# Context pass of the gated MLP: SiLU, product and rounding through PSUM, and row dots placed behind two merges

## The chip, the core and the metric

The kernel runs on one core of one Trainium2 chip. The metric is the device time of one launch, in microseconds (us). Five engines run their own instruction queues in order and wait for each other through semaphores: TensorE (PE, the matrix engine), VectorE (DVE), ScalarE (ACT), GpSimd (POOL) and SyncE (SP, here only a queue of transfers). SBUF is the working memory, PSUM the eight banks into which PE accumulates.

## The reference, cut to what matters

Two layers work on 1024 latent tokens and 256 context tokens, width 1024. The stage that is changed is the gated MLP of layer 0, which both kinds of tokens pass:

```python
def _conv_ffn(u, w_up, conv_w, w_down):
    gate, val = jnp.split(_dwconv3(u @ w_up, conv_w), 2, axis=-1)
    return (jax.nn.silu(gate) * val) @ w_down
```

`_dwconv3` is a depthwise convolution of width 3 over the tokens. The hidden width is 2816, which is 22 blocks of 128 (`FT`). Beside it the layer-1 modulation `silu(c) @ ada_w[1]` is computed, 64 row dots of 1024 by 1024 numbers each ("row dots").

## The kernel before, in words

`split_ffn_phase` is one of the phases that follow each other, each with one instruction list for each engine. Every float32 product is made of three passes of rounded operands: weights high times activation high, weights high times activation low, weights low times activation high. "High" is the rounded value, "low" the remainder that the rounding left. So each weight block is loaded, rounded by ACT (`c_high`, L2407) and its remainder is formed by POOL (L2230) or, for one block in three (`c_by_dve`), by DVE (L2553).

**The context pass** runs first. `C_STEPS` lists 66 products in the order gate f, value f, down f-1, each of 24 matmuls. The gate and value products of block f go in turn into three PSUM banks (`UP_BANKS`), of which they use columns 0 to 255. For each f, before the change: ACT scales the gate result by the centre tap into `c_gate` (L2418), DVE adds the two side taps (L871, L873), ACT makes SiLU in place in `c_gate` (L2421), ACT and DVE do the same for the value in `c_value` (L2424, L871, L873), DVE multiplies both into `c_value` (L2542), DVE casts the product into `c_act_hi` (L2546) and subtracts to get `c_act_lo` (L2548). These feed the down product one round later. `c_gate` and `c_value` exist once, so ACT holds the next centre tap until `c_mul` (L2418) or `c_ready` (L2424). For f = 1 to 16 a quarter of the norm work for the latent tokens (`dve_sums`, L1814 to L1844) stands on DVE behind the value step, and a few casts on ACT.

**The latent pass** follows: `ITEMS` is up 0, up 1, up 2, down 0, then up, up, down for nine groups, at last up 21, down 9 and the end. An up item is seven block products P1, P7, P6, P2, P5, P4, P3 of 12 matmuls, which DVE merges: U2 (L2568, needs P6), U3 (L2572, needs P7 and U2), C22 (L2576, P5), C21 (L2579, P4), C12 (L2582, P3). P4 reuses the bank of P7 and waits for U3; P3 waits for C22. If an up follows directly on an up, the elementwise tail of the one before is still pending: gate taps, `gated` (L2596), `rounded` (L2604) and `low` (L2608) stand on DVE around the first merges of the next. Each item also carries two row dots, a and b: ACT issues the load of a row tile into one single buffer (`act_load`, which waits until the dot before is done), and DVE multiplies and sums it (`dve_dot`, L1903). POOL forms the weight remainders (L2199) and the block sums (L2213 to L2224) through all of this.

## Time and profile before

| | us |
|---|---|
| median of three runs | 3247.65 (3243.78 to 3250.87) |
| the profiled execution | 3248.8 |
| its span | 3247.0 |
| context pass, first to last matmul | about 414.6 to 640 |
| latent pass of the same phase | about 640 to 1345 |
| PE busy over the span | 2983.1 (92%) |
| DVE busy | 2046.4 (63%) |
| ACT busy | 1174.5 (36%) |
| POOL busy | 1308.9 (40%) |
| mean granted TensorE clock | 0.964 of full |

The shares are means over stages of different kind. The views used are the waits (who waited for whom), the busy time by windows, and the order of single instructions in time. In a time line the first number is the start from the span's start, the second the length of the instruction or of the run of them (xN), and what stands in brackets is the idle time of the engine just before it and the instruction that ended it. A row by tile gives the shortest, median and longest length in ns.

### The profile page before, as it was taken

Reading aid. Unit: us, or ns where it says so; the run is one execution under the profiler, and the core shown is the slowest. Engines: PE = TensorE matmul, PEld = TensorE weight load, DVE = VectorE, ACT = ScalarE, POOL = GpSimd, SP = SyncE. Lnnn points to the kernel's source line nnn. Section 1 sums busy time; section 2 is a strip of 40 time slices with the busy share of each in tenths; the row PEclk is TensorE's granted clock in tenths of the full one; section 3 lists DMA queues with packets and bytes.
Section 4 is the critical chain, followed back from the end, with each engine's and each line's share of the span. In section 5 each row is a group of like instructions: output and inputs, shape, how many; then the busy total and the mean of one; then the engine's idle time right before and its main releaser. Section 6 shows DMA issues by size and latency. Waiting matters only on the chain. (4 is left out here: it accounts for less than half of the span.)

```text
span 3247.0 us, 67120 instructions
## 1 busy us (share of the span) xinstructions
PE 2983.1 (92%) x28494; PEld 2440.6 (75%) x28494; DVE 2046.4 (63%) x2839; ACT 1174.5 (36%) x2178; POOL 1308.9 (40%) x834
## 2 busy tenths in 40 slices
PE   6998998989999999889989979999987899999999
PEld 4655888877777777668877757777876678888887
DVE  4513489877777777831226757777765666656656
ACT  4011244332332233320025656666642433233232
POOL 3212054567766777343311100000004366566664
PEclk9998999999999999989989989999998999999999
DMA  5431044422233233212311011111012011111112
GB/s 233 151 120 39 27 132 155 163 94 89 97 104 101 88 104 104 72 65 78 106 63 57 16 35 29 30 32 38 24 36 96 22 57 57 48 52 65 39 52 78
DMA packets 135914, 247.36 MB, mean 76 GB/s; under 512 B 9537, under 2 KB 97985, under 8 KB 135490
## 3 DMA queue, kind: packets, MB, share of 16 engines
q1 hardware_dynamic: 97314, 193.92, 17.8%
q10 hardware_dynamic: 38304, 49.16, 4.4%
q8 instruction: 227, 3.72, 0.5%
q14 instruction: 69, 0.57, 0.1%
HBM read 221.15 MB, written 21.89 MB: 75 GB/s over the span
## 5 line engine op out<-in xcount | busy, mean ns | idle before, releaser
L1353 POOL TENSOR_TENSOR f_w_lo<-h,f_w_hi 128x512 fp32r<-128x512 f32 x92 | 139.2, 1522 | 149.4 <-ACT f_w_hi L1561 149.4
L3916 POOL TENSOR_TENSOR rw_inv_k<-rw_ss_k,rw_expo 128x4 f32<-128x4 f32 x20 | 20.2, 1010 | 440.0 <-ACT rw_ss_k L4219 440.0
L2199 POOL TENSOR_TENSOR f_w_lo<-f_u_hi_raw,f_w_hi 128x512 fp32r<-128x512 f32 x86 | 142.6, 1670 | 119.4 <-ACT f_w_hi L2440 119.4
L2230 POOL TENSOR_TENSOR c_lo<-c_raw,c_hi 128x1024 fp32r<-128x1024 f32 x45 | 110.9, 2484 | 195.5 <-ACT c_hi L2407 195.4
L2199 POOL TENSOR_TENSOR f_w_lo<-f_w_raw,f_w_hi 128x512 fp32r<-128x512 f32 x84 | 143.3, 1714 | 105.5 <-ACT f_w_hi L2440 105.5
L1429 PE MATMUL ps<-u_hi,f_w_hi 128*128 128x512 f32 x440 | 173.3, 394 | 9.2 <-DVE f_value L1674 4.3
L1429 PE MATMUL ps<-u_lo,f_w_hi 128*128 128x512 f32 x440 | 172.8, 393 | 0.0
L1429 PE MATMUL ps<-u_hi,f_w_lo 128*128 128x512 f32 x440 | 172.7, 392 | 0.0
L1353 POOL TENSOR_TENSOR f_w_lo<-f_w_raw,f_w_hi 128x512 fp32r<-128x512 f32 x84 | 126.5, 1515 | 96.2 <-ACT f_w_hi L1561 96.2
L167 PE MATMUL ps<-u_hi,w_hi 128*128 128x512 f32 x552 | 145.4, 370 | 6.5 <-ACT cd_stage L1027 6.5
L2327 PE MATMUL ps<-wn_t_hi,f_w_hi 128*128 128x512 f32 x264 | 112.1, 424 | 38.8 <-DVE f_value L2572 38.8
L167 PE MATMUL ps<-u_lo,w_hi 128*128 128x512 f32 x552 | 141.7, 363 | 0.0
L167 PE MATMUL ps<-u_hi,w_lo 128*128 128x512 f32 x552 | 141.5, 362 | 0.0
L155 POOL TENSOR_TENSOR w_hi<-w_raw,zero 128x1024 fp32r<-128x1024 f32 x28 | 54.6, 1950 | 211.5 <-PE ps L167 186.9
L2327 PE MATMUL ps<-u_hi,f_w_hi 128*128 128x512 f32 x352 | 137.0, 389 | 0.0
L871 DVE SCALAR_TENSOR_TENSOR cd_stage<-ps,small,cd_stage 128x1023 f32<-128x1023 f32 (+1 forms) x24 | 21.2, 883 | 183.8 <-ACT cd_stage L1020 183.3
L2327 PE MATMUL ps<-u_hi,f_w_lo 128*128 128x512 f32 x352 | 137.0, 389 | 0.0
L2327 PE MATMUL ps<-u_lo,f_w_hi 128*128 128x512 f32 x352 | 137.0, 389 | 0.0
L167 PEld LDWEIGHTS ps<-u_hi,w_hi 128*128 128x128 f32 x552 | 93.2, 190 | 47.5 <-issue 31.9
L4537 DVE TENSOR_TENSOR rw_px<-ps,rw_level 128x256 f32<-128x256 f32 x200 | 82.2, 417 | 73.8 <-PE ps L4088 73.3
L1903 DVE SCALAR_TENSOR_TENSOR h<-h 128x1024 f32<-128x1024 f32 x64 | 108.7, 1698 | 31.1 <-DMA h<-in_ada_rows 31.1
L2288 PE MATMUL ps<-u_hi,c_hi 128*128 128x256 f32 x352 | 102.9, 292 | 16.5 <-DVE c_lo L2553 16.5
(525 smaller groups left out, 9518.0 us busy)
## 6 DMA issues: line engine op xcount, KB each, us to landing
c_raw<-in_ffn SPq DMA_DIRECT2D x66, 512.0 KB, 3.5
f_w_raw<-in_ffn SPq DMA_DIRECT2D x64, 512.0 KB, 4.3
h<-in_ada_rows ACTq DMA_DIRECT2D x64, 512.0 KB, 3.9
h<-in_ffn SPq DMA_DIRECT2D x34, 512.0 KB, 4.8
f_u_hi_raw<-in_ffn SPq DMA_DIRECT2D x32, 512.0 KB, 4.9
ada_ring_s<-in_ada SPq DMA_DIRECT2D x22, 512.0 KB, 3.3
w_raw<-in_cd_in SPq DMA_DIRECT2D x20, 512.0 KB, 4.3
z_scratch<-cd_stage ACTq DMA_DIRECT2D x15, 640.0 KB, 5.5
```

The lines of the kernel that those rows point to most:

```text
L155: pool.tensor_tensor(hi, K.raw[:, raw, :], K.zero[:, 0:1].to_broadcast([P, KT * P]), ALU.add).then_inc(self.hi_done, 1)
L167: mm = pe.matmul(K.ps[:, slot, c, 0:width], wt[:, s, w], x[:, k, at:at + width], start=start and n == 0, stop=stop and n == 2)
L871: chain.link(dve.scalar_tensor_tensor(cv[:, at + 1:at + n], psum[:, at:at + n - 1], w0, cv[:, at + 1:at + n], ALU.mult, ALU.add))
L1353: pool.tensor_tensor(two(w_lo[n % RING]), source(x), two(w_hi[n % RING]), ALU.subtract).then_inc(w_split, 1)
L1429: mm = pe.matmul(o, wt, xt, start=t in OPENS and j == 0 and i == 0, stop=j == HK - 1 and i == 2, skip_group_check=t not in OPENS)
L1903: dve.scalar_tensor_tensor(self.tile, self.tile, 1.0, self.cond, ALU.mult, ALU.mult, accum_out=self.K.mod[:, 1, t, c:c + 1]).then_inc(self ...
L2199: pool.tensor_tensor(two(w_lo[n % RING][:, :]), source(x), two(w_hi[n % RING][:, :]), ALU.subtract).then_inc(w_split, 1)
L2230: pool.tensor_tensor(c_lo[n % LOWS][:, :], c_raw[n % LOWS][:, :], c_hi[n % HIGHS][:, :], ALU.subtract).then_inc(c_lo_pool, 1)
L2288: mm = pe.matmul(o, wt[:, w], x[:, k, gap], start=k == 0 and q == 0, stop=k == KT - 1 and q == 2)
L2327: mm = pe.matmul(o, wt, xt, start=t in OPENS and j == 0 and i == 0, stop=j == HK - 1 and i == 2, skip_group_check=t not in OPENS)
L3916: pool.tensor_tensor(R.inv[:, :], R.ss[:, :], R.expo[:, :], ALU.pow).then_inc(inv_done, 1)
L4537: dve.tensor_tensor(PX[:, s].rearrange("p (b h) c -> p b h c", b=2), banks(s)[:, :, 0:128].rearrange("p b (h c) -> p b h c", h=2), R.level ...
```

## The change

In the context pass SiLU is written to columns 256 to 511 of the gate's bank and the product to the same columns of the value's bank, so that both live in PSUM. The cast to `c_act_hi` moves from DVE to ACT. DVE's own remainder of a weight block comes ahead of the remainder of the activations. The waits follow: ACT's centre tap of the gate waits only for the SiLU before, that of the value for the product before, and PE's gate and value products wait for `c_ready` of two rounds before and `c_mul` of the round before, instead of `c_conv`. The split of the weight remainders (two of three on POOL) is as it was. In the latent pass the first row dot of an up item moves from before U2 to behind `low`, ahead of C22, and ACT issues the load of the second row tile at step P4 instead of P5.

```diff
+    def c_silu_at(f):
+        s, b = UP_BANKS[2 * f % UPS]
+        return K.ps[:, s, b, CTX:2 * CTX]
+
+    def c_gated(f):
+        s, b = UP_BANKS[(2 * f + 1) % UPS]
+        return K.ps[:, s, b, CTX:2 * CTX]
...
-                    if u >= UPS:
-                        pe.wait_ge(c_conv, u - UPS + 1)
+                    if kind == "gate" and f >= 2:
+                        pe.wait_ge(c_ready, f - 1)
+                    elif kind == "value" and f >= 1:
+                        pe.wait_ge(c_mul, f)
...
-                        pe.wait_ge(c_conv, 2 * FT)
+                        pe.wait_ge(c_ready, FT)
...
-                    act.wait_ge(c_mul, f)
+                    act.wait_ge(c_silu, f)
                     act.activation(c_gate[:, :], c_up(f, 0), ACT.Identity, scale=tap(1, 0, f)).then_inc(c_centre, 1)
...
-                    act.activation(c_gate[:, :], c_gate[:, :], ACT.Silu).then_inc(c_silu, 1)
+                    act.activation(c_silu_at(f), c_gate[:, :], ACT.Silu).then_inc(c_silu, 1)
                     act.wait_ge(c_done, n + 1)
-                    act.wait_ge(c_ready, f)
+                    act.wait_ge(c_mul, f)
...
+                if kind == "value":
+                    act.wait_ge(c_mul, f + 1)
+                    if f >= 2:
+                        act.wait_ge(c_done, C_NTH["down", f - 2] + 1)
+                    act.copy(c_act_hi[f % 2][:, :], c_gated(f)).then_inc(c_act_hi_done, 1)
...
                     if t == P5:
                         c11(n)
+                    if t == P4:
                         rows.act_load(act, b)
...
-                    dve.tensor_tensor(c_value[:, :], c_value[:, :], c_gate[:, :], ALU.mult).then_inc(c_mul, 1)
-                    dve.wait_ge(c_mul, f + 1)
-                    if f >= 2:
-                        dve.wait_ge(c_done, C_NTH["down", f - 2] + 1)
-                    dve.tensor_copy(c_act_hi[f % 2][:, :], c_value[:, :]).then_inc(c_act_hi_done, 1)
-                    dve.wait_ge(c_act_hi_done, f + 1)
-                    dve.tensor_tensor(c_act_lo[f % 2][:, :], c_value[:, :], c_act_hi[f % 2][:, :],
-                                      ALU.subtract).then_inc(c_ready, 1)
+                    dve.tensor_tensor(c_gated(f), c_value[:, :], c_silu_at(f), ALU.mult).then_inc(c_mul, 1)
                 if n + HIGHS < C_ALL and c_by_dve(n + HIGHS):
...
+                if kind == "value":
+                    dve.wait_ge(c_act_hi_done, f + 1)
+                    dve.tensor_tensor(c_act_lo[f % 2][:, :], c_gated(f), c_act_hi[f % 2][:, :],
+                                      ALU.subtract).then_inc(c_ready, 1)
...
-                    rows.dve_dot(dve, a)
                     merge(n, U2)
                     merge(n, U3)
                     if pending is not None:
                         low(pending)
+                    rows.dve_dot(dve, a)
                     merge(n, C22)
```

## Rows read from the trace of the kernel before

**Rows 1.** Windows: length, busy (count) of PE, PEld, DVE, ACT, POOL; clock; DMA.
```profile
472.00:494.00 22.00, 19.30 (x152) 18.17 (x151) 21.58 (x24) 10.72 (x16) 10.53 (x5) 1.00 0.47 154
604.00:626.00 22.00, 21.96 (x184) 22.00 (x185) 21.51 (x23) 11.12 (x16) 12.66 (x6) 1.00 0.60 197
837.20:840.10 2.90, 2.90 (x8) 2.32 (x7) 1.04 (x2) 1.21 (x2) 1.00 (x1) 0.50 0.87 291
842.00:856.00 14.00, 14.00 (x62) 11.44 (x61) 12.74 (x11) 3.99 (x4) 7.90 (x4) 1.00 0.34 112
```

**Rows 2.** Waits in the context pass (415 to 642): us in total, times, longest.
```profile
PE ps L2288 <- DVE c_lo L2553: 16.5, 16, 1.7
PE ps L2275 <- DVE c_act_lo L2548: 3.2, 4, 2.8
```

**Rows 3.** Time line of one round of the context pass, POOL and DVE.
```profile
513.92 4.96 POOL L2230 TENSOR_TENSOR c_lo<-c_raw,c_hi 128x1024 fp32r<-128x1024 f32 x2 [5.16 <-ACT c_hi L2407]
514.18 2.44 DVE L2542 TENSOR_TENSOR c_value<-c_value,c_gate 128x256 f32<-128x256 f32 x1
...
516.65 2.38 DVE L2546 CAST c_act_hi<-c_value 128x256 fp32r<-128x256 f32 x1
```

**Rows 4.** Time line of DVE late in the context pass, the product of two rounds.
```profile
615.19 2.44 DVE L2542 TENSOR_TENSOR c_value<-c_value,c_gate 128x256 f32<-128x256 f32 x1
...
623.51 2.44 DVE L2542 TENSOR_TENSOR c_value<-c_value,c_gate 128x256 f32<-128x256 f32 x1
```

**Rows 5.** Lengths by tile, context pass: count, min/median/max ns, first and last start.
```profile
L2230 POOL TENSOR_TENSOR c_lo<-c_raw,c_hi x45: 2379/2412/2608, 407.6 to 625.6; 128x1024 fp32r<-128x1024 f32 x45
L2553 DVE TENSOR_TENSOR c_lo<-c_raw,c_hi x21: 1212/1216/1217, 427.4 to 629.6; 128x1024 fp32r<-128x1024 f32 x21
...
L2424 ACT ACTIVATE c_value<-ps,small x22: 456/457/477, 421.6 to 630.1; 128x256 f32<-128x256 f32 x22
```

**Rows 6.** Lengths by line: a merge of the latent pass and the row dots.
```profile
L2572 DVE TENSOR_TENSOR f_value<-f_kept,ps x22: 686/687/689, 657.5 to 1314.1; 128x512 f32<-128x512 f32 x22
...
L1903 DVE SCALAR_TENSOR_TENSOR h<-h x64: 1206/1718/2309, 655.0 to 1340.8; 128x1024 f32<-128x1024 f32 x64
```

**Rows 7.** Time line of DVE, start of a first quarter of the norm work.
```profile
435.02 1.40 DVE L1814 SCALAR_TENSOR_TENSOR tn_t<-h,gs,ps 128x512 f32<-128x512 f32 x2
```

**Rows 8.** Time line of PE, last product of the context pass.
```profile
635.71 0.46 PE L2275 MATMUL ps<-c_act_hi,c_hi 128*128 128x256 f32 x1 [2.76 <-DVE c_act_lo L2548]
```

**Rows 9.** Waits of PE in the latent pass (642 to 1345).
```profile
PE ps L2327 <- DVE f_value L2572: 38.8, 13, 4.4
```

**Rows 10.** Time lines of POOL, DVE and PE, up 6 of the latent pass.
```profile
830.51 3.52 POOL L2199 TENSOR_TENSOR f_w_lo<-f_u_hi_raw,f_w_hi 128x512 fp32r<-128x512 f32 x2 [2.76 <-ACT f_w_hi L2440]
833.99 2.25 POOL L2199 TENSOR_TENSOR f_w_lo<-f_w_raw,f_w_hi 128x512 fp32r<-128x512 f32 x1
...
831.22 1.67 DVE L2604 CAST u_lo<-f_gate 128x1024 fp32r<-128x1024 f32 x1
832.81 2.30 DVE L1903 SCALAR_TENSOR_TENSOR h<-h 128x1024 f32<-128x1024 f32 x1
...
835.82 0.69 DVE L2572 TENSOR_TENSOR f_value<-f_kept,ps 128x512 f32<-128x512 f32 x1
836.43 1.22 DVE L2608 TENSOR_TENSOR u_lo<-f_gate,u_lo 128x1024 fp32r<-128x1024 f32 x1
837.56 0.68 DVE L2576 TENSOR_TENSOR f_value<-f_value,ps 128x512 f32<-128x512 f32 x1
841.28 0.69 DVE L2579 TENSOR_TENSOR f_value<-f_kept,ps 128x512 f32<-128x512 f32 x1 [3.03 <-PE ps L2327]
...
836.65 0.47 PE L2327 MATMUL ps<-wn_t_hi,f_w_hi 128*128 128x512 f32 x1 [2.80 <-DVE f_value L2572]
```

**Rows 11.** Time line of DVE, up 0 of the latent pass.
```profile
655.02 1.74 DVE L1903 SCALAR_TENSOR_TENSOR h<-h 128x1024 f32<-128x1024 f32 x1 [11.45 <-DMA h<-in_ada_rows]
...
663.57 0.69 DVE L2579 TENSOR_TENSOR f_value<-f_kept,ps 128x512 f32<-128x512 f32 x1 [4.62 <-PE ps L2327]
```

**Rows 12.** DMA issues: transfer, queue, count, size, median us to landing.
```profile
h<-in_ada_rows ACTq DMA_DIRECT2D x64, 512.0 KB, 3.9
```

## The prediction, made before the changed kernel ran

> **What bounds the kernel now.** I read the windows first. Before the norm quarters end, PE issues 152 matmuls in 22 us of the context pass, so the 72 of one f (gate, value, down) take 72 x 22 / 152 = 10.42 us. After they end it is 184 in 22 us, 8.61 us per f, and PE has no idle time left: that is PE's own pace. In both stretches DVE is busy for over 21.5 of the 22 us and the clock is full [rows 1]. So DVE bounds the 16 rounds f = 3 to 18, which carry most of the 16 quarters, and PE and DVE about meet behind them. The waits say the same: PE waits 16 times for DVE's remainder of the weights, 16.5 us, and once 2.8 us for `c_act_lo` of the last f [rows 2, 8]. The listed waits are shorter than the difference (1.8 us per f), because PE also restarts slowly behind each.
>
> Why DVE is full shows in single instructions. A 128x256 product takes 2.44 us and the cast behind it 2.38 us. Each begins beside one of POOL's two remainders of a weight block (2.4 us each, 4.96 us together) and ends right behind it [rows 3, 5]. The same engine does four times the elements in 1.216 us [rows 5]. So these two do not compute for 4.8 us, they wait: DVE instructions that read only SBUF and POOL's instructions exclude each other. A merge that takes one operand from PSUM does not wait: 686 to 689 ns in all 22 cases, beside a busy POOL or not [rows 6]. A row dot, all in SBUF, has 1206 to 2309 ns [rows 6].
>
> In the latent pass PE waits 13 times for U3 (L2572), 38.8 us in all [rows 9]. In order of time: `rounded`, then the row dot with 2.30 us (half of it a wait for POOL), then U2 and U3, then P4 begins 2.80 us late [rows 10]. Behind that gap the clock is 0.50, the lower of its levels, 1.2 GHz in place of 2.4; a full-clock window has 62 matmuls in 14 us, 0.226 us each [rows 1]. P4's merge C21 starts 841.28 - 836.65 = 4.63 us after P4 starts [rows 10], against 12 x 0.226 = 2.7 and about 0.2 of latency, so each gap costs another 1.7 us. The context pass has gaps of up to 1.7 us (1.9 with the usual distance of matmuls) and keeps the clock at 1.00 [rows 1, 2]. Up 0 is a case of its own: the dot waits for its tile until 655.02 and holds U2 and U3 behind it (the one wait of 4.4 us) [rows 9, 11].
>
> **Context pass, per f.** DVE's round without quarters is 623.51 - 615.19 = 8.32 us [rows 4]. The change removes 2.44 + 2.38 = 4.82 and some 0.06 of starts: 3.44 remain (four side taps, its own weight remainder, `c_act_lo`). It adds the product with one operand in PSUM. Between 512 elements with a PSUM operand (0.687) and 1024 in SBUF (1.216) lie 1.03 ns per element [rows 5, 6], so 256 take 0.42 us. It adds a wait for ACT's copy, priced as ACT's 128x256 from PSUM, 0.46 us [rows 5], with about 0.2 us of two handovers: 0.65. Queued behind that wait on DVE are `c_act_lo` and the quarter. Sum 4.5 us. ACT stands at 10.7 busy of 22 us [rows 1]; one copy for each f is free there.
>
> The quarter costs 10.42 - 8.32 = 2.1 us. Before, it ran while POOL idled, starved by DVE; now it meets POOL's two instructions, since PE and ACT hand out blocks faster. I laid one round out with these lengths: counted from the end of a value product, ACT's centre tap and cast let POOL start near 1.6 us, and `c_act_lo` ends near 3.2 us. The quarter's first SBUF-only instruction then meets the rest of POOL's first (about 0.7 us), and as the two engines alternate, its second meets the whole of POOL's second (2.4 us): 3.1. In one quarter of four, the first two instructions read PSUM (1.40 us, two of them [rows 7]), which leaves about 1.7. Mean (3 x 3.1 + 1.7) / 4 = 2.8. DVE's round is then 4.5 + 2.1 + 2.8 = 9.4 us: still above PE's 8.61, so DVE stays the bound, with small gaps on PE, and 10.42 - 9.4 = 1.0 us per f is won, 16 x 1.02 = 16.3 us. The last down product waited 2.76 us [rows 8] behind product, cast and subtraction; the new chain behind the last value product (centre, taps, product, copy, low: about 3.3 us) is hidden by the down product between (24 x 0.12 = 2.9) but for 0.4: 2.4 us. Context pass: **19 us**.
>
> Bounds. Without any waits for POOL, PE's 8.61 holds: 16 x 1.8 + 2.8 = 32 us won. With two whole POOL instructions waited for in each f (it issues no more), 4.5 + 2.1 + 4.8 = 11.4, 16 us lost less 2.4: 13 us slower. The new waits of PE (`c_ready` two rounds back, `c_mul` one round back) were signalled over 4 us earlier in that layout and cost nothing; if DVE fell behind, they would be what PE shows. POOL's instruction count is unchanged.
>
> No row has a DVE or ACT instruction that writes PSUM beside POOL. I take them as unheld, from the merges that read it (0.687); held, the product costs up to 2.4. The page "SBUF — State Buffer" of the Trainium skill (Who interferes with whom) says that a VectorE instruction with at most one SBUF input and outside its two-port modes never meets GpSimd. Against the change speaks another page of the Trainium skill, "VectorE: DVE Perf Modes" (The TRN2 errata): a PSUM source costs 120 cycles of fixed time where an SBUF source costs 58, an estimate of 0.065 us for each of two instructions, 2.8 us over 22 rounds. The rows do not show it: 0.687 us at 512 elements with PSUM is what the SBUF row gives (1.216 less 512 x 1.03 ns).
>
> **Latent pass, per up.** Take up 6 [rows 10]. `rounded` ends at 832.8. U2 and U3 follow at once, 0.78 + 0.69: U3 ends at 834.3 (before 836.5), and P4 starts at 834.4 instead of 836.65, 0.7 us after PE is free (836.65 - 2.80 - 0.15 = 833.7). But DVE's work has only been turned round: `low` (1.22) and the dot (1.21 alone [rows 6]) now stand ahead of C22. POOL takes the port at 833.99 for 1.3 us, `low` runs to 836.4, the dot to 837.6, C22 to 838.3. P4 is done at 837.1, so P3 waits 1.2 us for C22, which it did not before. P3 starts at 838.4; before, it started as P4 ended, at 841.1. **2.7 us** are won, of 4.5 that gap and clock cost. Two gaps of 0.7 and 1.2 us should leave the clock full, as in the context pass [rows 1, 2].
>
> I count eight such ups (every second one, 65 us apart). Four (1, 2, 20, 21) stand in a row of three ups, where POOL goes on with the next up's sums and `low` and dot can each meet one more instruction of 1.3 us; there 1.4 to 3.0, taken as 2.2. In up 0 the dot still starts at 655.02 when its tile lands, but P4 no longer waits. C22 ends at 657.4, C21 starts there instead of at 663.57 [rows 11]: 6.1 us. Sum 6.1 + 8 x 2.7 + 4 x 2.2 = **36.5 us**. In ups without a pending tail the dot fits into DVE's idle time before C22. The second tile's load goes out one product later and behind the first dot, at about the time when it did before, since ACT was held by `low` until then. It lands 3.9 us later [rows 12], while C22, C21, the centre tap, two side taps and C12 stand ahead of its dot (3 x 0.69 + 3 x 1.2 = 5.7 us). Bounds: all gaps and slow stretches gone, 38.8 + 13 x 1.7 = 61 us; nothing won if P3 waits so long that the clock falls there instead.
>
> **Sum.** 3248.8 - 19 - 36.5 = 3193 us for the profiled execution, which is 1.2 us above the median of the runs; I give **3193**. Behind the pass all engines start relative to its end, and nothing there is changed.
>
> **Rivals.**
> (a) More is won. The quarters meet POOL less than laid out; towards PE's pace that is up to 13 us more in the context pass, and less contention in the latent pass: around 3178. For it: PE's pace of 8.61 has been reached [rows 1]. Against it: the port is wanted for 4.8 us by POOL and about 3 by DVE in each f.
> (b) The wait at C22 takes the place of that at U3. `low` and the dot each meet a POOL instruction, P3 waits 2.5 us and the clock falls over P3 (1.7 us) in most of twelve ups: the latent pass wins about 18 instead of 36.5: 3211. For it: this very clock fall behind a wait of 2.80 us. Against it: POOL idles after 836.2 in the steady groups [rows 10].
> (c) PSUM does not free the product. Operands or output in PSUM still hold the port in the context pass; DVE's round is about 11.4 us, 13 us lost there, latent as forecast: 3225. Against it: 22 merges within 3 ns.
> (d) The change does not act: the dots are bound by their transfers and PE by something that the waits do not name; within 5 us of 3248. Against it: DVE's waits of 4.8 us in each f are plain rows.
> (e) Slower. Port waits at their most in both passes: POOL, no longer starved, is inside an instruction each time that an SBUF-only one of DVE comes. 13 us lost in the context pass, and in the latent pass C22 up to 1.3 us later than before with P3 at the low clock: level or some 1 us lost for an up: 3262. It decides from a DVE round of over 10.4 us and C22 later than 3.4 us after P4's start. Against it: POOL's count is fixed, and it is busy for under half of the time [rows 1].
>
> **How the numbers follow.** Forecast 0.60 (3183 to 3203 its own range), (a) 0.15, (b) 0.14, (c) 0.05, (d) 0.02, (e) 0.04. The range takes in most of (a) and (b): 3175 to 3213. A measurement of this kernel can tell about 0.2% (6.5 us) from no change. Faster by more: all of forecast, (a), (b), (c): 0.94. Same 0.02, slower 0.04.
>
> **What would show it.** The product (new line of L2542) at about 0.42 us and never over 1; ACT's copy near 0.46; SBUF-only instructions of the quarters at up to 3.1 us; PE windows in the context pass at about 168 matmuls for 22 us; the last down product waiting under 1 us. In the latent pass: waits of PE for U3 under 1 us, new waits of PE for C22 (L2576's line) of about 1.2 us each, clock 1.00 where it was 0.50. Wrong would be: 152 matmuls or fewer for 22 us, the clock at 0.50 behind C22, or DVE waiting for the second row tile.

## The result, and the profile after

The changed kernel takes 3197.64 us (median of four runs, 3193.64 to 3198.39) against 3249.1 us of the kernel before (median of four, 3243.78 to 3250.87). The ratio is 0.9842, with 0.9825 to 0.9859 as its 95% interval. That is 51.5 us or 1.6% faster. 3193 was forecast, and 3183 to 3203 as the forecast's own range.

The profiled execution has a span of 3195.6 us. To see where the time went, I cut the span of both profiles at four marks that PE's matmuls give (the first of the context pass, the first of the latent pass, the first and the last of the end item), and did the same for every experiment below:

| us | to the first context product | context pass | latent pass | products of the end item | rest | span |
|---|---|---|---|---|---|---|
| before | 414.6 | 225.5 | 704.1 | 28.7 | 1874.1 | 3247.0 |
| after | 414.3 | 199.4 | 675.7 | 28.1 | 1878.1 | 3195.6 |
| difference | -0.3 | **-26.1** | **-28.4** | -0.6 | +4.0 | -51.4 |

19 and 36.5 us were forecast for the two passes. Their sum, 55.5, was met (54.5, and 55.4 with the small ends), but the two terms were not: one was 7 us too small, the other 8 us too large. The 4.0 us in the rest lie in phases whose code is the same. The whole table of experiments shows that such stretches differ from one execution to the next (see "What the runs showed").

The engines' totals on the page of the kernel after:

```profile
PE 2968.5 (93%) x28494; PEld 2428.6 (76%) x28494; DVE 1991.8 (62%) x2817; ACT 1177.7 (37%) x2200; POOL 1289.6 (40%) x834
```

DVE lost 54.6 us of busy time (2046.4 before). Only one instruction for each of the 22 blocks went, the cast (2839 - 2817 = 22), which is 6.4 us at the 0.29 us that it takes where nothing holds it (e10 below). Most of the rest was waiting inside instructions, which the profile counts as busy.

**Context pass.** Windows of after: length, busy (count) of PE, PEld, DVE, ACT, POOL; clock; DMA. The first answers to [rows 1], the other two belong to the latent pass:

```profile
472.00:494.00 22.00, 21.34 (x174) 20.61 (x172) 20.80 (x28) 12.98 (x21) 10.77 (x5) 1.00 0.53 174
656.00:658.00 2.00, 2.00 (x6) 1.57 (x6) 0.00 (x0) 1.04 (x2) 2.00 (x2) 0.52 0.68 233
799.00:803.00 4.00, 3.19 (x13) 2.37 (x14) 4.00 (x5) 1.38 (x3) 1.65 (x2) 1.00 0.66 227
```

174 matmuls in the 22 us instead of 152, which is 72 x 22 / 174 = 9.1 us per f. Lengths in the context pass of after (count, min/median/max ns, first and last start) are the product, ACT's new copy and the subtraction:

```profile
L2560 DVE TENSOR_TENSOR ps<-c_value,ps x22: 428/429/430, 422.8 to 609.3; 128x256 f32<-128x256 f32 x22
...
L2443 ACT CAST c_act_hi<-ps x22: 372/373/375, 423.3 to 609.8; 128x256 fp32r<-128x256 f32 x22
...
L2568 DVE TENSOR_TENSOR c_act_lo<-ps,c_act_hi x22: 424/425/427, 423.7 to 610.2; 128x256 fp32r<-128x256 f32 x22
```

The product that took 2.44 us in [rows 3] takes 0.43 us, 22 times within 2 ns. In 21 of the 22 cases POOL is inside a remainder all the while, as it was before. The time line of one round, DVE and then POOL (start, length, what stood idle before it):

```profile
503.08 0.43 DVE L2560 TENSOR_TENSOR ps<-c_value,ps 128x256 f32<-128x256 f32 x1
...
503.94 0.42 DVE L2568 TENSOR_TENSOR c_act_lo<-ps,c_act_hi 128x256 fp32r<-128x256 f32 x1 [0.44 <-ACT c_act_hi L2443]
504.29 1.40 DVE L1814 SCALAR_TENSOR_TENSOR tn_t<-h,gs,ps 128x512 f32<-128x512 f32 x2
505.72 2.45 DVE L1817 SCALAR_TENSOR_TENSOR wn_u_full<-tn_t,mod,u_hi 128x512 f32<-128x512 f32 x1
...
513.10 1.50 DVE L1823 SCALAR_TENSOR_TENSOR wn_t_full<-tn_t,mod,wn_u_full 128x512 f32<-128x512 f32 x1
514.51 2.90 DVE L1826 SCALAR_TENSOR_TENSOR u_lo<-tn_t,mod,u_hi 128x512 fp32r<-128x512 f32 x1
...
502.83 4.79 POOL L2240 TENSOR_TENSOR c_lo<-c_raw,c_hi 128x1024 fp32r<-128x1024 f32 x2 [3.89 <-ACT c_hi L2419]
...
511.63 5.23 POOL L2240 TENSOR_TENSOR c_lo<-c_raw,c_hi 128x1024 fp32r<-128x1024 f32 x2 [4.01 <-ACT c_hi L2419]
```

POOL runs from 502.83 to 507.62. ("The port" stands below for what a DVE instruction with its operands in SBUF and an instruction of POOL can't have at the same time.) The product, the subtraction and the two L1814, which all have an operand in PSUM, run through at full speed. L1817 reads SBUF alone: it begins at 505.72 and ends only at 508.17, 0.55 us behind POOL. In the kernel before, where the quarters ran while POOL was idle, L1817 has 0.75 us, so 1.7 us of it are waiting. In the next quarter the first such instruction waits for 0.75 us (1.50 in all) and the second for 2.15 us (2.90). The contention did not vanish. It moved from the product and the cast onto the quarters, as laid out, in size too.

**Latent pass.** PE's waits there (total us, times, longest), for U3 and C22; the third row is the context pass:

```profile
PE ps L2339 <- DVE f_value L2587: 13.8, 12, 2.5
PE ps L2339 <- DVE f_value L2591: 11.3, 11, 1.9
PE ps L2300 <- DVE c_lo L2564: 1.9, 3, 0.7
```

38.8 us for U3 in [rows 9] have become 13.8, and 11.3 for C22 are new. The wait for `c_lo` in the context pass fell from 16.5 us [rows 2] to 1.9. Up 6 again, as [rows 10] show it of before: DVE, POOL, PE.

```profile
795.78 1.66 DVE L2619 CAST u_lo<-f_gate 128x1024 fp32r<-128x1024 f32 x1
797.37 0.67 DVE L2583 TENSOR_TENSOR f_kept<-f_kept,ps 128x512 f32<-128x512 f32 x1
798.15 0.69 DVE L2587 TENSOR_TENSOR f_value<-f_kept,ps 128x512 f32<-128x512 f32 x1
798.75 2.15 DVE L2623 TENSOR_TENSOR u_lo<-f_gate,u_lo 128x1024 fp32r<-128x1024 f32 x1
800.83 1.21 DVE L1903 SCALAR_TENSOR_TENSOR h<-h 128x1024 f32<-128x1024 f32 x1
...
801.97 0.67 DVE L2591 TENSOR_TENSOR f_value<-f_value,ps 128x512 f32<-128x512 f32 x1
...
798.54 1.28 POOL L2209 TENSOR_TENSOR f_w_lo<-f_w_raw,f_w_hi 128x512 fp32r<-128x512 f32 x1
...
798.98 0.47 PE L2339 MATMUL ps<-wn_t_hi,f_w_hi 128*128 128x512 f32 x1 [0.92 <-DVE f_value L2587]
...
802.79 0.47 PE L2339 MATMUL ps<-u_hi,f_w_hi 128*128 128x512 f32 x1 [0.81 <-DVE f_value L2591]
```

The order is the one laid out, and `low` (L2623) meets one POOL instruction. P4 is 0.92 us late and P3 0.81, and the clock stays at 1.00 over both and behind them (windows 799 to 803 and 660 to 1260).

### The profile page after: what moved, and what is told of

Same layout as the page of the kernel before. It is cut to its first block and busy times, and to the rows that moved or that the text cites. A ratio compares the mean times of both kernels' runs of the same rounds, so it can differ in the third digit from the quotient of the medians.

```text
span 3195.6 us, 67120 instructions
## 1 busy us (share of the span) xinstructions
PE 2968.5 (93%) x28494; PEld 2428.6 (76%) x28494; DVE 1991.8 (62%) x2817; ACT 1177.7 (37%) x2200; POOL 1289.6 (40%) x834
## 5 line engine op out<-in xcount | busy, mean ns | idle before, releaser
L2209 POOL TENSOR_TENSOR f_w_lo<-f_u_hi_raw,f_w_hi 128x512 fp32r<-128x512 f32 x86 | 129.3, 1514 | 118.8 <-ACT f_w_hi L2457 118.8
L1353 POOL TENSOR_TENSOR f_w_lo<-f_w_raw,f_w_hi 128x512 fp32r<-128x512 f32 x84 | 127.0, 1520 | 96.5 <-ACT f_w_hi L1561 96.5
L2209 POOL TENSOR_TENSOR f_w_lo<-f_w_raw,f_w_hi 128x512 fp32r<-128x512 f32 x84 | 125.9, 1508 | 98.6 <-ACT f_w_hi L2457 98.6
L2339 PE MATMUL ps<-u_hi,f_w_hi 128*128 128x512 f32 x352 | 138.3, 393 | 11.3 <-DVE f_value L2591 11.3
L155 POOL TENSOR_TENSOR w_hi<-w_raw,zero 128x1024 fp32r<-128x1024 f32 x28 | 54.6, 1950 | 210.9 <-PE ps L167 187.0
L871 DVE SCALAR_TENSOR_TENSOR cd_stage<-ps,small,cd_stage 128x1023 f32<-128x1023 f32 (+1 forms) x24 | 21.2, 883 | 184.0 <-ACT cd_stage L1020 183.6
L2339 PE MATMUL ps<-wn_t_hi,f_w_hi 128*128 128x512 f32 x264 | 104.5, 396 | 14.7 <-DVE f_value L2587 13.8
L1710 DVE SCALAR_TENSOR_TENSOR h<-ps,mod,h 128x1024 f32<-128x1024 f32 x80 | 99.5, 1277 | 23.4 <-PE ps L1508 23.4
L2629 DVE SCALAR_TENSOR_TENSOR h<-ps,mod,h 128x1024 f32<-128x1024 f32 x80 | 100.5, 1276 | 20.6 <-PE ps L2362 20.6
```

The costliest lines, as they stand in the source:

```text
L155: pool.tensor_tensor(hi, K.raw[:, raw, :], K.zero[:, 0:1].to_broadcast([P, KT * P]), ALU.add).then_inc(self.hi_done, 1)
L1353: pool.tensor_tensor(two(w_lo[n % RING]), source(x), two(w_hi[n % RING]), ALU.subtract).then_inc(w_split, 1)
L1710: dve.scalar_tensor_tensor(K.h[:, m, 0:SEQ].rearrange("p (b c) -> p b c", b=2), K.ps[:, s, b:b + 2, :], K.part(layer, 5, m, 0), K.h[:, m, ...
L2209: pool.tensor_tensor(two(w_lo[n % RING][:, :]), source(x), two(w_hi[n % RING][:, :]), ALU.subtract).then_inc(w_split, 1)
L2339: mm = pe.matmul(o, wt, xt, start=t in OPENS and j == 0 and i == 0, stop=j == HK - 1 and i == 2, skip_group_check=t not in OPENS)
L2629: dve.scalar_tensor_tensor(two(K.h[:, m, 0:SEQ]), K.ps[:, s, b:b + 2, :], K.part(layer, 5, m, 0), two(K.h[:, m, 0:SEQ]), ALU.mult, ALU.add ...
```

## The experiments

The same cuts through every profile, in us:

| | to context | context pass | latent pass | end item | rest | median |
|---|---|---|---|---|---|---|
| e1_context_only | 408.2 | 199.4 | 704.7 | 26.4 | 1870.2 | 3220.62 |
| e2_dots_only | 408.8 | 224.0 | 676.1 | 29.5 | 1870.7 | 3215.50 |
| e3_sbuf_cast_on_act | 411.2 | 223.4 | 675.3 | 27.8 | 1875.1 | 3215.82 |
| e4_merges_first | 409.6 | 199.4 | 662.8 | 30.4 | 1870.3 | 3178.32 |
| e5_c22_first | 412.5 | 199.5 | 668.6 | 28.0 | 1875.0 | 3185.36 (one) |
| e6_all_on_pool | 407.9 | 231.3 | 675.9 | 29.3 | 1868.0 | 3214.21 (one) |
| e7_two_on_dve | 412.9 | 191.4 | 676.0 | 29.3 | 1877.4 | 3188.81 (one) |
| e8_load_at_p5 | 413.2 | 199.5 | 676.4 | 30.1 | 1878.3 | 3199.28 (one) |
| e9_merges_first_two_on_dve | 415.1 | 191.4 | 662.7 | 32.0 | 1874.3 | 3176.91 |
| e10_before_two_on_dve | 412.7 | 209.0 | 703.5 | 28.6 | 1873.9 | 3229.58 (one) |
| e11_centre_before_casts | 414.4 | 191.5 | 663.2 | 31.6 | 1870.5 | 3171.96 |
| e12_centre_first_in_threes | 413.6 | 191.5 | 659.9 | 31.4 | 1874.8 | 3171.54 |

"One" marks a kernel with a single time. Read the middle columns: kernels with the same code in a pass agree there within 1.5 us.

### The two parts by themselves (e1, e2)

e1 is the changed kernel with the latent pass of before (dot a ahead of U2, load at P5). e2 is the kernel before with only this edit:

```diff
                     if t == P5:
                         c11(n)
+                    if t == P4:
                         rows.act_load(act, b)
...
-                    rows.dve_dot(dve, a)
                     merge(n, U2)
                     merge(n, U3)
                     if pending is not None:
                         low(pending)
+                    rows.dve_dot(dve, a)
                     merge(n, C22)
```

> The context part alone; the row dots and the load of the second tile stand as before. My theory (both parts act by themselves): the first latent matmul comes near 614 us instead of 640.1, the latent pass keeps its 13 waits for U3 of 38.8 us, total 26 us below the kernel before, near 3223. Rival (the two parts depend on each other, for example because the context pass changes where the latent pass starts against its transfers): the latent pass changes too, by more than 3 us.

> The latent part alone. My theory: the context pass ends at 640 us as before, PE's waits for U3 fall from 38.8 us to about 14, new waits for C22 of about 11 us appear, total 25 to 29 us below the kernel before, near 3222. It also tells whether the 3 to 4 us that the changed kernel lost behind this phase (between 1904 and 2520 us in the trace of before) come with one part: my theory says that they belong to neither and vary with the execution; the rival says that they follow an earlier or denser PE.

Measured: 0.9923 of before (0.9906 to 0.994) and 0.9912 (0.9892 to 0.9932). PE's waits, of e1 in the latent pass and of e2 in both:

```profile
PE ps L2339 <- DVE f_value L2586: 38.2, 13, 4.5
```

```profile
PE ps L2288 <- DVE c_lo L2554: 16.4, 16, 1.7
PE ps L2327 <- DVE f_value L2573: 15.1, 12, 2.3
PE ps L2327 <- DVE f_value L2577: 9.8, 11, 1.9
```

Each kernel has the waits of before in the pass that it leaves alone and those of after in the other. The context part gives 26.1 us (225.5 - 199.4), and its latent pass is within 0.6 us of before. The latent part gives 28.0 us, and its context pass is within 1.5 us. So the parts add up, and neither pays for the other. The rest is 1870.2 and 1870.7 us, so neither part brings the 4.0 us by which after's is longer than before's.

### Is it PSUM, or the cast's move to ACT? (e3)

The changed kernel, with SiLU and product in two new SBUF tiles. The cast stays on ACT, the order on all engines is that of after, and each of the two tiles has one wait more for its reuse:

```diff
 def c_silu_at(f):
-    s, b = UP_BANKS[2 * f % UPS]
-    return K.ps[:, s, b, CTX:2 * CTX]
+    return c_silu_tile[:, :]
...
 def c_gated(f):
-    s, b = UP_BANKS[(2 * f + 1) % UPS]
-    return K.ps[:, s, b, CTX:2 * CTX]
+    return c_gated_tile[:, :]
...
+                    act.wait_ge(c_mul, f)
                     act.activation(c_silu_at(f), c_gate[:, :], ACT.Silu).then_inc(c_silu, 1)
...
+                    dve.wait_ge(c_ready, f)
                     dve.tensor_tensor(c_gated(f), c_value[:, :], c_silu_at(f), ALU.mult).then_inc(c_mul, 1)
```

> The changed kernel with SiLU and the product in two SBUF tiles of their own in place of PSUM; the cast stays on ACT, the order is the same. My theory (PSUM is what frees the product and the remainder from the port that DVE shares with POOL): the product waits for POOL's first remainder again (near 2.4 us instead of 0.43) and the subtraction for its second (up to 2.8 instead of 0.42); DVE's round is near 10 us and the context pass wins at most 8 of its 26 us: total near 3217. Rival (the cast's move to ACT is what gives the gain): total as the changed kernel, near 3198.

Measured: 223.4 us for the context pass, 2.1 less than before, where PSUM gives 26.1. Lengths by tile of e3, product and subtraction:

```profile
L2562 DVE TENSOR_TENSOR c_gated_t<-c_value,c_silu_t x22: 426/2430/2624, 419.7 to 630.2; 128x256 f32<-128x256 f32 x22
...
L2570 DVE TENSOR_TENSOR c_act_lo<-c_gated_t,c_act_hi x22: 424/426/430, 422.8 to 631.1; 128x256 fp32r<-128x256 f32 x22
```

The product is back at a median of 2430 ns and has its computing time of 426 ns only in the one case where POOL is idle. So the place of operands and output frees it, not the new order: 24 of the 26.1 us. The subtraction was expected to wait for POOL's second remainder and does not. That shows nothing about the port: POOL is idle at all 22 of its turns, since its two instructions are not back to back in e3. The second one meets a quarter's instruction instead (L1826 takes 2.93 us behind it, 0.74 without a wait). In this time line the product ends at 524.8, behind a single instruction of POOL that ends at 524.5:

```profile
522.12 2.40 POOL L2240 TENSOR_TENSOR c_lo<-c_raw,c_hi 128x1024 fp32r<-128x1024 f32 x1 [4.01 <-ACT c_hi L2419]
522.37 2.43 DVE L2562 TENSOR_TENSOR c_gated_t<-c_value,c_silu_t 128x256 f32<-128x256 f32 x1
```

The two subtraction rows, that of e3 (SBUF source, 424/426/430 ns) and that of after (PSUM source, 424/425/427 ns), also settle the objection in the prediction, whose own check was circular: its 1.03 ns per element had been drawn from the two rows that it was then said to fit. The page "VectorE: DVE Perf Modes" of the Trainium skill (The TRN2 errata) makes a PSUM source dearer by 62 cycles. These rows show no difference. The page "SBUF — State Buffer" of the Trainium skill (Who interferes with whom) says that a DVE instruction with at most one SBUF input doesn't contend with GpSimd, and that one with two contends with a GpSimd instruction that reads SBUF. The trace agrees: with one, 21 products beside POOL took 428 to 430 ns, and with two, in e3, all 21 beside POOL were held.

### How much of the round is the port? (e6, e7, e10)

The number of POOL's remainders per f is the dose: two in after, three in e6, one in e7. e10 is the kernel before with the line of e7.

```diff
 def c_by_dve(n):
-    return n % 3 == 2 and n > 2
+    return n < 0                  # e6
+    return n % 3 != 0 and n > 2   # e7, e10
```

> The changed kernel with all three weight remainders of a round on POOL, none on DVE. My theory (in the rounds with norm quarters DVE is bound by its waits for POOL's 2.4 us instructions): POOL is busy 7.2 us of each round and each SBUF-only instruction of DVE meets one, so rounds grow from 9.2 to 11 or 12 us and the context pass (first context to first latent matmul, 199.4 us) to 225 to 238. Rival (DVE is bound by its own work): DVE has 1.2 us less in each round, rounds near 8.6 us, 190 us.

> The changed kernel with two of three weight remainders on DVE and one on POOL. My theory (waits for the port bound DVE): DVE gains 1.2 us of work in each round but loses most of its 2.7 us of waits, rounds at PE's own 8.6 us, context pass near 190 us instead of 199.4. Rival (DVE's own work bounds): rounds of 10.4 us, context pass near 218 us.

> The kernel before (product and cast in SBUF on DVE) with two of three remainders on DVE. It asks whether the port could have been freed without PSUM. My theory: the product still meets POOL's one instruction (2.4 us) but the cast no longer does (0.3): a round loses 2.1 us of wait and gains 1.2 us of work, so it falls from 10.5 to about 9.6 us and the context pass from 225 to about 210. Rival: the two waits were the only thing that counted and one remains, with 1.2 us of work on top: no gain, 225 or more.

Measured, context pass with three, two and one remainder on POOL: 231.3, 199.4, 191.4 us. e6 is slower there than the kernel before, although DVE has 1.2 us less to compute for each f than in after. Its wait, its window, and the time line of one round:

```profile
PE ps L2300 <- POOL c_lo L2240: 27.3, 15, 3.0
```

```profile
472.00:494.00 22.00, 19.11 (x145) 18.71 (x145) 19.21 (x19) 9.85 (x16) 15.41 (x7) 0.92 0.44 144
```

```profile
501.43 7.25 DVE L1844 TENSOR_TENSOR wn_t_lo<-wn_t_full,wn_t_hi 128x512 fp32r<-128x512 f32 x3
...
500.16 7.97 POOL L2240 TENSOR_TENSOR c_lo<-c_raw,c_hi 128x1024 fp32r<-128x1024 f32 x3 [3.89 <-ACT c_hi L2419]
```

Three instructions of a quarter take 7.25 us: each ends behind one of POOL's three. PE now waits for POOL, and the clock is at its lower level for 3.4 us of this window, which makes its mean 0.92. This is rival (e), a POOL that is inside an instruction whenever DVE comes, and it needs a third remainder to decide: with two it does not. In e7 PE has no wait in the context pass, and its window is full:

```profile
472.00:494.00 22.00, 22.00 (x187) 22.00 (x186) 20.66 (x30) 13.20 (x20) 6.05 (x3) 1.00 0.54 176
```

187 matmuls are 8.5 us per f, PE's own pace. That the window before had DVE full at 21.58 and this one has it at 20.66 with one more remainder (1.2 us) of its own shows what DVE's busy time was: waits. e10 gives 16.5 us without touching the product. Its time line, POOL and DVE:

```profile
504.36 2.42 POOL L2230 TENSOR_TENSOR c_lo<-c_raw,c_hi 128x1024 fp32r<-128x1024 f32 x1 [6.76 <-ACT c_hi L2407]
...
504.60 2.45 DVE L2542 TENSOR_TENSOR c_value<-c_value,c_gate 128x256 f32<-128x256 f32 x1
...
507.08 0.29 DVE L2546 CAST c_act_hi<-c_value 128x256 fp32r<-128x256 f32 x1
```

The product still waits for POOL's only instruction, but the cast takes 0.29 us instead of 2.38 [rows 3], since no second one follows. So 16.5 of the 26.1 us could have been had by relieving POOL alone, and both edits together give 34.1 (e7).

### What holds C22 and U3? (e4, e5, e8)

e4 also takes `rounded` behind U3 and puts both `low` and the dot behind C22. e5 only moves C22 ahead of `low` and the dot. e8 leaves the second tile's load at P5.

```diff
                         gated(pending)
-                        rounded(pending)
                     merge(n, U2)
                     merge(n, U3)
                     if pending is not None:
+                        rounded(pending)
+                    merge(n, C22)
+                    if pending is not None:
                         low(pending)
                     rows.dve_dot(dve, a)
-                    merge(n, C22)
                     merge(n, C21)
```

> The changed kernel with DVE's list of an up item in the order gated, U2, U3, rounded, C22, low, dot, C21: the pending tail's cast behind U3, and C22 ahead of low and the dot. My theory (what is left of PE's waits in the latent pass is DVE's order, not its load): both waits (U3 13.8 us, C22 11.3 us) go in the eight steady groups, about 2 us for a group, and some in the rows of three ups: total 15 to 22 us below the changed kernel, near 3180. Rival (the rounded values come later and the wait moves to the products that need them, or to ACT's copy of C11): the same total within 5 us, with a new wait of PE in P1 or the down items.

> The changed kernel with C22 ahead of low and the first row dot (order U2, U3, C22, low, dot, C21), rounded as it was. My theory: the wait for C22 (11.3 us in 11 ups) goes, that for U3 (13.8 us) stays; latent pass from 675.7 us to about 667. Rival: low is now 0.7 us later and ACT's copy of C11 and the casts behind it hold PE instead; latent pass within 2 us of 675.7.

> The changed kernel with the load of the second row tile back at step P5; the dots stay behind the merges. My theory: ACT then waits for the first dot ahead of the cast for the down items' or the next up's operands, but that cast has slack; latent pass within 2 us of 675.7. Rival (the move of the load is a needed part): the cast comes late, POOL and PE behind it wait, latent pass longer by 5 us or more.

Measured: e4 is at 0.9796 of before (0.9778 to 0.9814); its latent pass has 12.9 us less than after's. e5 has 7.1 us less, e8 has 0.7 more, within what repeats. So the load's move to P4 is no needed part of the change. PE's waits in the latent pass, of e5 and then of e4:

```profile
PE ps L2339 <- DVE f_value L2587: 18.6, 12, 2.6
```

```profile
PE ps L2362 <- POOL f_w_lo L2209: 3.9, 10, 0.6
PE ps L2339 <- POOL f_w_lo L2209: 3.4, 3, 1.4
PE ps L2339 <- ACT f_kept L2463: 3.3, 2, 1.7
PE ps L2362 <- DVE h L2629: 2.6, 9, 0.3
PE ps L2339 <- DVE f_value L2587: 2.0, 3, 0.9
```

In e5 the wait for C22 is gone, but the one for U3, which was expected to stay, grew from 13.8 to 18.6: PE now reaches the next U3 earlier, and `rounded` still stands before it. In e4 both are gone (2.0 us left of 25.1). In their place come some 0.6 us for each down item (L2362), whose products wait for a remainder of POOL's and for DVE's adding of the down products, 3.3 us for ACT's copy `f_kept` and 2.6 us more for POOL's remainders in ups (0.8 in after): 12.4 us in all. So 23.1 us of waits less are 10.7 net, and the pass is 12.9 us shorter. The rest fits the clock, which is full through the whole pass in e4 and at its lower level twice for 3.4 us in after (an estimate: 1.7 us of full-clock work lost each time). In the steady groups the time from C21 to C21 over one group (up, up, down) is 64.9 us before, 62.5 after and 61.4 in e4.

### Both together, and the rows of three ups (e9, e11, e12)

After's latent pass has its longest waits in the rows of three ups. Time line of up 1 of after, DVE, POOL and PE (P4, then P3):

```profile
649.91 2.15 DVE L2623 TENSOR_TENSOR f_act_lo<-f_gate,f_act_hi 128x1024 fp32r<-128x1024 f32 x1
651.98 2.31 DVE L1903 SCALAR_TENSOR_TENSOR h<-h 128x1024 f32<-128x1024 f32 x1
...
649.70 1.28 POOL L2223 TENSOR_TENSOR f_s<-f_u_hi_raw 128x512 f32<-128x512 f32 x1
...
651.06 2.15 POOL L2226 TENSOR_TENSOR f_u_hi_raw<-f_u_hi_raw 128x512 f32<-128x512 f32 x1
...
650.14 0.47 PE L2339 MATMUL ps<-wn_t_hi,f_w_hi 128*128 128x512 f32 x1 [2.53 <-DVE f_value L2587]
...
655.04 0.47 PE L2339 MATMUL ps<-u_hi,f_w_hi 128*128 128x512 f32 x1 [1.93 <-DVE f_value L2591]
```

Here `low` and the dot each meet a POOL instruction (2.15 and 2.31 us, where 1.22 and 1.21 are their own), so C22 is late and P3 waits 1.93 us for it. In up 20 it is 1.95 us, with the same two lengths (2.16 and 2.31). Behind P3's wait in up 1 the clock falls (0.52, window 656 to 658 above). The 2.53 us before P4 come from further back, from the tail of up 0. Its time line, ACT and DVE:

```profile
633.18 0.62 ACT L2457 CAST f_w_hi<-f_w_raw 128x512 fp32r<-128x512 f32 x1 [3.95 <-POOL f_w_raw L2230]
634.89 1.77 DVE L2603 SCALAR_TENSOR_TENSOR f_cv<-f_value,small,f_cv 128x1023 f32<-128x1023 f32 x1 [2.87 <-ACT f_cv L2475]
```

ACT's cast of a weight block sum stands ahead of the centre tap `f_cv`. It waits 3.95 us for POOL's sum, and DVE, which has nothing else, waits 2.87 us for the tap. Up 1 (3.17 us, at 658.66) and up 20 (3.18 us, at 1244.92) have the same wait of DVE. What DVE does for the next up is late by the part of it that is not usual: elsewhere DVE waits some 1.25 us for the tap (up 19, at 1221.12). P4 of up 1 and of up 21 (2.28 us) wait for it; in up 2 PE is late itself, and P4 waits only 0.74 us. e9 is e4 with e7's line; e11 adds the tap ahead of the casts at each up that an up follows; e12 does so only at ups 0, 1 and 20:

```diff
             for i, x in enumerate(STEPS):
-                highs_before(i)
                 kind, n, t = x
+                early = kind == "up" and t == P3 and i + 1 < len(STEPS) and STEPS[i + 1][0] == "up"  # e11
+                early = kind == "up" and t == P3 and n in (0, 1, FT - 2)                               # e12
+                if early:
+                    centre_value(n)
+                highs_before(i)
...
-                        centre_value(n)
+                        if not early:
+                            centre_value(n)
```

> Both remedies together on the changed kernel: DVE's order of the latent pass (gated, U2, U3, rounded, C22, low, dot, C21) and two of three weight remainders on DVE. My theory (two separate passes, each with its own bound): the gains add, context pass near 191.4 us, latent pass near 662.8 us, total 8 us below the kernel with the order alone, 70 to 80 us below the kernel before, near 3170. Rival: the start or the end of the phase takes some of it back.

> The same as the kernel with both remedies, and in an up item that is followed by an up ACT makes the value's centre tap before the casts of step P3. It asks where the rest of the forecast in the rows of three ups went. My theory: in these ups ACT's cast waits for POOL's last block sum and the centre tap behind it comes 2 to 3 us late, which lengthens DVE's round; with the centre tap first the latent pass falls from 662.8 us by 3 to 8 us. Rival (the casts come too late for PE): new waits of PE for POOL's remainders in steps P1 to P6, latent pass the same or longer.

> The kernel with both remedies, with ACT's centre tap ahead of the casts only in ups 0, 1 and 20, whose tail is pending in a row of three ups. In the version that did it in every up followed by an up, the distance from C21 to C21 fell from 22.3 and 22.7 us to 22.1 and 21.3 in the rows of three, and grew by 0.4 us in the nine pairs. My theory: without the pairs only the gain is left, about 3 us: latent pass near 660 us against 662.7, context pass 191.4. Rival: the gain in the rows of three is taken back by the items behind them; latent pass 662 to 664 us.

Measured: 0.9791 (0.9769 to 0.9814), 0.9779 (0.9759 to 0.9799) and 0.9743 (0.9715 to 0.977) of before. e9 has the context pass of e7 and the latent pass of e4, to 0.1 us. But its total, expected 8 us below e4's, is only 1.4 us below (0.9791 of before against 0.9796). In the profiled executions its stretch ahead of the context pass is 5.5 us longer and its rest 4.0, neither of which it touches, and its end item is 1.6 us longer. A part of what is won in the passes may be given back in the end item, where PE waits for the norm of the next phase, twice (`tn_acc`, L411): 6.2 us in after, 7.5 in e4 and 8.2 in e9. No run tests that.

e11 wins 1.4 us from C21 of up 1 to that of up 2 and again from up 20 to up 21 (22.7 to 21.26 and to 21.24), and gives it back in the nine steady pairs, where one group goes from 61.4 to 61.8 us, since the casts come later there. The pass is where it was, 663.2, and the 3 to 8 us that were expected are missed. e12 keeps only the first half and has the shortest pass, 659.9 (from C21 of up 0 to that of up 1 it is 0.4 us longer than e9). ACT and DVE of e12 at up 0:

```profile
623.45 1.15 ACT L2475 ACTIVATE f_cv<-f_value,small 128x1024 f32<-128x1024 f32 x1 [2.82 <-DVE f_value L2598]
624.54 0.62 ACT L2457 CAST f_w_hi<-f_w_raw 128x512 fp32r<-128x512 f32 x1
624.64 2.13 DVE L2607 SCALAR_TENSOR_TENSOR f_cv<-f_value,small,f_cv 128x1023 f32<-128x1023 f32 x1 [1.22 <-ACT f_cv L2475]
```

The tap now waits for the merge before it, not for POOL, and DVE for 1.22 us instead of 2.87. e12's median of 3171.54 us stands against 3253.18 of the kernel before in the same comparison: 81.6 us or 2.6% faster, against 51.5 us for the change. The kernel before is slow in that comparison, though: in e11's it had 3241.42, and e11's own median is within 0.5 us of e12's. From the profiled spans, 3247.0 and 3171.2 us, e12 wins 75.8.

## Why the prediction was right, and where it was not

**Context pass, mechanism: right.** DVE waited for POOL in product and cast, and PSUM frees the product: 428 to 430 ns in 22 cases, 21 of them beside POOL, where 0.42 us was forecast, and 2430 again in e3. Rival (c) is out by that. Rival (d) is out by e1 and e2, which each win. Rival (a), with PE near its own pace, did not come: the window has 174 matmuls, not 184. It takes one remainder less on POOL (e7).

**Context pass, size: 26.1 us instead of 19.** Four terms of the sum were off, each by a little:
- The round before was taken from one window as 10.42 us. Over the 16 rounds with a quarter DVE's gate taps (L871) lie 10.56 us apart.
- The round after was put at 9.4 us. By the same taps it is 9.26. ACT's copy takes 373 ns and DVE waits 0.44 us for it, where 0.65 was priced from an activation of the same shape with a tap. The port waits of the quarters, laid out as 1.7 for one in four and 3.1 for the others, are 1.7, 2.9 and 3.0: this step held.
- Both make it 1.30 us per f in place of 1.02, 20.8 us in 16 rounds. The stretch before the quarters set in gives another 0.9 us and the four rounds behind them 1.3, which the sum left out.
- From the last gate tap to the end of the pass 3.1 us were won, against 2.4 for the last product.

For the same reason the bound of 32 us for a pass without waits was too low: e7 wins 34.1.

**Latent pass, steady ups: the layout held, the price was a little high.** P4 was put at 0.7 us late and is 0.92; P3 at 1.2 and is 0.81; the clock stays full, the point on which rival (b) hung. From C21 to C21 the eight groups give 2.46 us each in the mean against 2.7 forecast: 19.7 us against 21.6. Up 0 gives 5.8 against 6.1.

**Latent pass, rows of three ups: this step failed.** Four ups were to give 2.2 us each, 8.8 in all. From C21 to C21 ups 1 and 2 give 0.2 and 1.2 us, ups 20 and 21 give 1.3 and 0.2: 2.8 in all. I had looked there for `low` and the dot meeting POOL, and in ups 1 and 20 they do: P3 waits 1.93 and 1.95 us for C22, against 0.81 in the steady groups. What I had not looked at is who is late once DVE's order is mended: the centre tap on ACT, behind a cast that waits for POOL's last block sum. So P4 is 2.53 us late in up 1 and 2.28 in up 21, not 0.92. The clock does fall twice, at 656 us behind P3's wait in up 1 and at 1260 us behind P4's in up 21. In up 1 that is rival (b) with its own cause and the late tap on top; in up 21 only the tap is late. e11 and e12 show what the tap is worth, but in e4's order of DVE: with the tap ahead of the cast, and nothing else changed, e12's pass is 2.8 us shorter than e9's. How the missing 6.0 us divide in the order of after isn't shown.

**The end.** "Behind the pass all engines start relative to its end" holds for the code but not for a comparison of two executions: 4.0 us were lost there. Without them the profile would have shown 3193.4 us.

**The total** of 3197.64 is 4.6 us above the forecast, but it is partly luck: +7 and -8 us in two terms cancelled. A sum that fits says less than its terms do.

## What to carry to other kernels

When an instruction of DVE takes several times what its elements cost, and ends right behind one of POOL's, count what POOL runs there before counting what DVE computes: either give the instruction an operand in PSUM (here an input and the output) or give POOL less, and expect the remaining SBUF-only instructions to inherit the waits. When an order on one engine is mended, ask which engine feeds the new first instruction and what it waits for: here it was a tap that stood behind another cast, in the places that won least. Put merges that free a bank ahead of everything that only prepares the next stage, all of them and not only the first ones: U2 and U3 ahead of the dot (the change) gave 28 us, all three merges ahead of `low` and the dot and the first two ahead of `rounded` as well (e4) 41.

## What the runs showed of the hardware

- **An instruction of DVE and one of POOL that both need the port take turns.** A DVE instruction that comes while POOL is inside one waits for its end (0.75 us and 1.7 us above), then runs; the next one waits for the whole of POOL's next (2.15 us of 2.4). A triple takes 7.25 us beside a triple of POOL's (e6). A short instruction of DVE pays as much as a long one: 0.29 us of cast become 2.38.
- **Where the clock fell.** It stayed at 1.00, the 2.4 GHz level, through all the steady groups of after, with gaps of 0.92 and 0.81 us (3.0 us from the restart to the next gap). How long a single wait is did not settle it: behind waits of 2.53 us (up 1 of after, P4) and 3.01 us (e6, at 502.56) the clock stayed full for the next 2 us, and it fell to 0.50, the 1.2 GHz level, behind the 1.93 us that followed on the 2.53, behind 2.28 us (after, up 21) and behind 2.12 us (e7, at 640.41). Each of these falls lasted 3.4 us.
- **Untouched phases differ between executions by more than some edits are worth.** The stretch ahead of the context pass has 407.9 to 415.1 us over the fourteen profiles, the rest 1868.0 to 1878.3, though the code there is the same in all, while the two passes repeat within 1.5 us. An edit of some microseconds is better read from its own stretch than from the total.
